# Merge products of two decoder layers taken as three products of split parts instead of one fp32 product

## What is computed

```python
yA = silu(layernorm(conv(...))) @ w_conv_out          # (264 x 512) @ (512 x 1024)
yB = (rmsnorm(o) * silu(z)) @ w_delta_out             # (264 x 512) @ (512 x 1024)
merged = sigmoid(p_gateA) * yA + sigmoid(p_gateB) * yB
x = x + merged @ w_o                                  # (264 x 1024) @ (1024 x 1024)
x = x + FFN(rmsnorm(x))                               # dense in layer 0, top-2-of-8 experts in layer 1
```

## Time and profile before

| | us |
|---|---|
| median of three runs | 1575.98 |
| the profiled execution | 1574.31 |
| its span in the profile | 1572.5 |
| merge stage, layer 0 (first merge product to first output product) | 224.29 to 263.22 |
| merge stage, layer 1 | 697.01 to 735.95 |

### The profile page before, as it was taken

How to read it: one execution, slowest core, us unless ns; L and a number is a source line. 1 busy time by engine, 2 the same in 40 slices (tenths; PEclk the granted TensorE clock), 3 DMA queues, 4 the chain that set the end, 5 groups by cost and what they waited for, 6 DMA issues and landing times.

```text
span 1572.5 us, 31141 instructions
## 1 busy us (share of the span) xinstructions
PE 1539.2 (98%) x11103; PEld 1398.9 (89%) x11103; DVE 1259.7 (80%) x1813; ACT 964.8 (61%) x1340; POOL 46.0 (3%) x52
## 2 busy tenths in 40 slices
PE   7999899999999999999999999999999999999997
PEld 6989887999998989987898997989979899898995
DVE  5878965655545878965598999989899998998987
ACT  5643442544435643442477777777778777787775
POOL 0000000000000000000060000000000000000000
PEclk9999899999999999899999999999999999999999
DMA  7642224687555642234599999999999999999993
GB/s 278 192 102 68 68 86 162 223 272 245 177 168 173 198 102 68 56 91 169 201 354 390 379 358 373 351 360 359 364 371 350 364 358 365 357 349 375 356 366 114
DMA packets 109040, 397.54 MB, mean 253 GB/s; under 512 B 13617, under 2 KB 13664, under 8 KB 108448
## 3 DMA queue, kind: packets, MB, share of 16 engines
q1 hardware_dynamic: 104608, 376.23, 68.1%
q0 software_dynamic: 4352, 20.20, 4.0%
HBM read 380.94 MB, written 16.43 MB: 253 GB/s over the span
## 4 chain that ended last, share of the span: by engine, by line
PE 90%; DVE 8%; ACT 1%; issue 1%; DMA 0%; SPq 0%; DVEq 0%; ACTq 0%
PE psum L1443 74%; DVE c L1011 3%; PE psum L1665 2%; PE psum L1667 2%; PE psum L1558 1%; PE psum L1566 1%; PE psum L1456 1%; PE psum L1674 1%; PE psum L1835 1%; PE psum L1570 1%; DVE w_lo L894 1%; PE psum L1524 1%; PE psum L1788 1%; PE psum L1464 1%; PE psum L1789 0%
## 5 line engine op out<-in xcount | busy, mean ns | idle before, releaser
L1443 PE MATMUL psum<-w_hi,h_hi 128*96 128x256 f32 x1408 | 399.9, 284 | 0.9 <-DVE w_lo L1381 0.9
L1443 PE MATMUL psum<-w_hi,h_lo 128*96 128x256 f32 x1408 | 394.5, 280 | 0.0
L1443 PE MATMUL psum<-w_lo,h_hi 128*96 128x256 f32 x1408 | 393.7, 280 | 0.0
L1381 DVE TENSOR_TENSOR w_lo<-ring,w_hi 128x1024 fp32r<-128x1024 f32 x288 | 346.7, 1221 | 37.2 <-ACT w_hi L847 35.1
L847 ACT ACTIVATE w_hi<-ring 128x1024 fp32r<-128x1024 f32 x288 | 303.6, 1058 | 42.9 <-PE psum L1443 34.0
L1443 PE MATMUL psum<-hid_hi,w_hi 128*128 128x264 f32 x1072 | 312.6, 292 | 1.0 <-DVE hT L1197 0.8
L1443 PE MATMUL psum<-hid_lo,w_hi 128*128 128x264 f32 x1072 | 306.4, 286 | 0.0
L1443 PE MATMUL psum<-hid_hi,w_lo 128*128 128x264 f32 x1072 | 306.0, 285 | 0.0
L582 ACT ACTIVATE w_hi<-ring 128x1024 fp32r<-128x1024 f32 x156 | 164.2, 1056 | 162.8 <-PE psum L1443 123.3
L894 DVE TENSOR_TENSOR w_lo<-ring,w_hi 128x1024 fp32r<-128x1024 f32 x156 | 189.3, 1218 | 92.5 <-ACT w_hi L582 92.3
L1381 DVE TENSOR_TENSOR w_lo<-early,w_hi 128x1024 fp32r<-128x1024 f32 x192 | 231.3, 1221 | 17.9 <-ACT w_hi L847 17.8
(11 more groups left out here) (335 smaller groups left out, 1958.1 us busy)
## 6 DMA issues: line engine op xcount, KB each, us to landing
ring<-in_w_exp SPq DMA_DIRECT2D x288, 512.0 KB, 5.5
early<-in_w_exp SPq DMA_DIRECT2D x192, 512.0 KB, 5.4
ring<-in_w_mixer SPq DMA_DIRECT2D x112, 512.0 KB, 3.6
ring<-in_w_ffn SPq DMA_DIRECT2D x66, 512.0 KB, 4.5
qkv<-in_w_exp SPq DMA_DIRECT2D x48, 512.0 KB, 5.6
h_rows<-work POOLq DMA_DIRECT2D x12, 480.0 KB, 5.1
early<-in_s POOLq DMA_DIRECT2D x2, 2048.0 KB, 8.3
out_ss<-early POOLq DMA_DIRECT2D x2, 2048.0 KB, 9.4
```

Source lines behind the costliest of these rows:

```text
L1381: V.tensor_tensor(w_lo[:, buffer_x(u), :], slot_x(u % RING_X), w_hi[:, buffer_x(u), :], ALU.subtract).then_inc(lo_done, 1)
L1443: last = M(out, lhs[x], rhs[w], start=(start and n == 0), stop=(stop and n == 2))
```

## The change

The eight merge tiles of each layer join the split tiles. ACT makes high parts of `c` (a second silu with a reduced output, ahead of the one in place) and of `o` (four copies), DVE makes their low parts, in work space that is free by then. High and low parts of tiles 40 to 47 are made as of any other tile, three ahead, so that in every turn of the merge loop ACT now makes the high part of tile 43 + t and DVE its low part at the end of the turn. PE takes 24 split products a tile in place of 16 full ones, and waits at its first two merge tiles only for the gates whose banks they overwrite (37 for the first, 39 for the second), and at each tile of `c` and `o` for its low part.

```diff
--- before.py
+++ after.py
@@ -172,6 +172,19 @@
 
         def glu_gate(j):
             return work[:, 8, (j % 2) * T:(j % 2 + 1) * T]
+
+        mix_a = work_r[:, 5:8, :].rearrange("p a b -> p (a b)")
+        mix_b = work_r[:, 0:2, :].rearrange("p a b -> p (a b)")
+
+        def o_part(lo, h):
+
+            return mix_a[:, (4 * lo + h) * T:(4 * lo + h + 1) * T]
+
+        def c_part(lo, j):
+
+            if lo and j == 3:
+                return mix_a[:, 8 * T:9 * T]
+            return mix_b[:, (4 * lo + j) * T:(4 * lo + j + 1) * T]
 
         vmask = units(4)
         sq_o = work[:, 0:2, :].rearrange("p a b -> p (a b)")[:, 0:H * T].rearrange("p (h t) -> p h t", t=T)
@@ -317,6 +330,9 @@
         ln_var = sem("ln_var")
         ln_norm = sem("ln_norm")
         c_done = sem("c_done")
+        o_hi_done = sem("o_hi_done")
+        c_lo_done = sem("c_lo_done")
+        o_lo_done = sem("o_lo_done")
         merged_done = sem("merged_done")
         x_done = sem("x_done")
         silu_done = sem("silu_done")
@@ -382,9 +398,9 @@
 
 
         split_ord = {}
-        for section, tiles in (("mix0", [i for i in range(N_PROJ) if i not in PLAIN]), ("mix0", range(N_PROJ + N_MIX, N_LAYER)),
+        for section, tiles in (("mix0", [i for i in range(N_PROJ) if i not in PLAIN]), ("mix0", range(N_PROJ, N_LAYER)),
                                ("ffn", range(2, N_FFN)),
-                               ("mix1", [i for i in range(N_PROJ) if i not in PLAIN]), ("mix1", range(N_PROJ + N_MIX, N_LAYER))):
+                               ("mix1", [i for i in range(N_PROJ) if i not in PLAIN]), ("mix1", range(N_PROJ, N_LAYER))):
             for i in tiles:
                 split_ord[first_position(section) + i] = len(split_ord)
         split_at = {v: k for k, v in split_ord.items()}
@@ -717,8 +733,7 @@
                             act.wait_ge(qconv_done, 6 * (l + 1))
                             act.wait_ge(qk_state_out, 16 * 2 * (l + 1))
                         A(gs[:, t, :], psum[:, (GATE_AT + t) % 4, 0:T], ACT.Sigmoid).then_inc(act_evac, 1)
-                        if GATE_AT + t + LEAD < N_PROJ:
-                            high_part(section, GATE_AT + t + LEAD)
+                        high_part(section, GATE_AT + t + LEAD)
 
                 z_silu(0)
                 silu_qkv(4, 8)
@@ -764,14 +779,17 @@
                 warm(ACT.Silu)
                 for j in range(CT):
                     act.wait_ge(ln_norm, CT * l + j + 1)
+                    A(c_part(0, j), c[:, j, :], ACT.Silu, scale=par("ln_g", l * CT + j), bias=par("ln_b", l * CT + j))
                     A(c[:, j, :], c[:, j, :], ACT.Silu, scale=par("ln_g", l * CT + j), bias=par("ln_b", l * CT + j)).then_inc(c_done, 1)
+                act.wait_ge(o_done, l + 1)
+                for h in range(H):
+                    A(o_part(0, h), qkv[:, 8 + h, :], ACT.Copy).then_inc(o_hi_done, 1)
                 gates(14, 16)
 
                 for k in range(KD):
                     act.wait_ge(merged_done, KD * l + k + 1)
                     A(x_hi[:, k, :], hT[:, k, :], ACT.Copy).then_inc(x_hi_done, 1)
-                    if k < LEAD:
-                        high_part(f"mix{l}", N_PROJ + N_MIX + k)
+                    high_part(section, N_PROJ + LEAD + k)
                 for t in range(LEAD, N_WO):
                     high_part(f"mix{l}", N_PROJ + N_MIX + t)
                 if l:
@@ -1188,6 +1206,15 @@
                 o_all = qkv[:, 2 * H:3 * H, :]
                 settle(V.scalar_tensor_tensor(o_all, o_all, par("o_g", l), psum[:, 4:8, 0:T], ALU.mult, ALU.mult))
                 V.tensor_tensor(o_all, o_all, zs[:, :, :], ALU.mult).then_inc(o_done, 1)
+                low_part(section, N_PROJ)
+                for j in range(CT):
+                    dve.wait_ge(c_done, CT * l + j + 1)
+                    V.tensor_tensor(c_part(1, j), c[:, j, :], c_part(0, j), ALU.subtract).then_inc(c_lo_done, 1)
+                for h in range(H):
+                    dve.wait_ge(o_hi_done, H * l + h + 1)
+                    V.tensor_tensor(o_part(1, h), qkv[:, 8 + h, :], o_part(0, h), ALU.subtract).then_inc(o_lo_done, 1)
+                for t in range(1, LEAD):
+                    low_part(section, N_PROJ + t)
                 dve.wait_ge(s0_scaled, l + 1)
 
                 for t in range(KD):
@@ -1200,8 +1227,7 @@
                     dve.wait_ge(outer_mm, 8 * l + t + 1)
                     blk = s0[:, 4 * t:4 * t + 4, :].rearrange("p u d -> p (u d)")
                     V.tensor_tensor(blk, blk, psum[:, 6 + t % 2, :], ALU.add).then_inc(outer_taken, 1)
-                    if t >= KD - LEAD:
-                        low_part(f"mix{l}", N_PROJ + N_MIX + t - KD + LEAD)
+                    low_part(section, N_PROJ + LEAD + t)
                 x_low(3 * l + 1, KD - 1)
                 for t in range(KD):
                     dve.wait_ge(units_used, base_ord[f"mix{l}"] + N_PROJ + N_MIX + t + 1)
@@ -1653,18 +1679,18 @@
                 spread(o_rstd, H, 0)
                 project(38)
                 project(39)
-                pe.wait_ge(act_evac, 32 * (l + 1))
-
-                pe.wait_ge(o_done, l + 1)
-                pe.wait_ge(c_done, CT * (l + 1))
                 for t in range(KD):
-                    w = arrived(section, N_PROJ + t)
-                    if t >= 2:
+                    w = parts(section, N_PROJ + t)
+                    if t < 2:
+                        pe.wait_ge(*freed(l, N_PROJ - 3 + 2 * t))
+                    else:
                         pe.wait_ge(merged_done, KD * l + t - 1)
                     for j in range(CT):
-                        M(psum[:, 2 * (t % 2), 0:T], w[:, j, :], c[:, j, :], start=(j == 0), stop=(j == CT - 1))
+                        pe.wait_ge(c_lo_done, CT * l + j + 1)
+                        split_products(psum[:, 2 * (t % 2), 0:T], [x[:, j, :] for x in w], [c_part(0, j), c_part(1, j)], j == 0, j == CT - 1)
                     for h in range(H):
-                        last = M(psum[:, 2 * (t % 2) + 1, 0:T], w[:, CT + h, :], qkv[:, 8 + h, :], start=(h == 0), stop=(h == H - 1))
+                        pe.wait_ge(o_lo_done, H * l + h + 1)
+                        last = split_products(psum[:, 2 * (t % 2) + 1, 0:T], [x[:, CT + h, :] for x in w], [o_part(0, h), o_part(1, h)], h == 0, h == H - 1)
                     last.then_inc(units_used, 1)
                     if t == 0:
                         pe.wait_ge(samp_vm, l + 1)
```

## The result

The changed kernel takes 1565.67 us as the median of eight runs (1561.6 to 1569.62), the kernel before 1576.12 (eight runs, 1573.58 to 1580.13): a ratio of 0.9926 (95% interval 0.9912 to 0.9939), or 9.6 to 13.9 us less. On another occasion, on one chip with three further kernels, it was 1566.16 against 1577.56 us, 0.9932 (0.9913 to 0.9952). The forecast was 1566.8 us, 9.2 less. The profiled span fell from 1572.5 to 1563.2 us.

What follows compares the result with a forecast made beforehand. PE was taken to bound the merge stages, with the DVE-ACT loop narrowly setting their end after the change. 2 x 4.6 = 9.2 us off the profiled 1574.31 gives 1565.1; the median's 1.67 more makes 1566.8 us, range 1563.5 to 1571.5.

Steps and rivals of the forecast that it cites:

- PE's part: Merge tile on PE: 2.90 us split products, 0.20 switching, 1.05 outer product, 4.15 us in all instead of 4.80.
- The bound of 4.46: Upper bound for PE's merge tile, with both the 0.20 us and the 0.31 us switching costs counted.
- The start: First merge tiles: the 0.48 us wait for the last gate goes; the second tile begins 0.5 us late, at 228.2.
- rival (c): Late start: ACT's table switch behind the copies takes twice 1.28 us, everything behind comes 1.3 us later; 1569.4 us, chance 0.02.
- The loop: Merge turns: DVE's merge, ACT's `x_hi` and high part, DVE's low part make a 3.93 us round that sets the end.
- rival (e): Slower: DVE's 0.94 us falls behind ACT's high part, round 4.87; stage loses from 4.6 on; 1580.0 us, chance 0.06.
- Narrowly: End of merge: the DVE-ACT round, done at 258.2 us, sets the end rather than PE, which would allow 257.5.
- The first output tile: Behind the merge: starts at 258.2 us, 5.0 earlier, but waits 0.4 us for the last `x_lo`.
- The sum: Both merge stages: 4.6 us a layer, 9.2 us in all, giving 1566.8 us.
- Rival (a): PE's products alone decide: 0.85 us comes back in each of 16 merge tiles, 13.6 us, 1562.4 us; chance 0.08.
- Rival (d): Given back: something behind the merge, a load or the norm, keeps its own time; 1576 us, chance 0.06.

Runs made afterwards that it cites:

- split outer: Changed kernel with high part ahead of the merge, second tile's high part and last `x_lo` earlier, outer product as three split products; 1566.08 us, 0.9923 to the kernel before.
- the copies inside: Changed kernel plus two 256-column ACT copies in every merge turn, between `x_hi` and the high part; 1577.6 us, 0.9999 to the kernel before.
- the short outer product: Changed kernel with the outer product cut to 128 of 512 columns, rest of the state update left out; 1568.8 us, 0.995 to the kernel before.
- the shorter wait alone: Kernel before with only the shorter wait for gates at the first two merge tiles, products left whole; 1578.98 us, 1.0002 to the kernel before.

## Why the prediction was right

**PE's part.** 4.15 us a tile was taken, with 0.20 for switching and the outer product's 1.05 as it stood. Where PE sets the pace the runs show 4.14 to 4.18. The 0.20 was right as a price, but not as one of switching between full and split products, as split outer shows. The bound of 4.46 rests on a miscount: a merge tile held eight full products and not 16, since each shows as two records, so that one takes 3.75/8 = 0.47 us (and three of split parts, 0.36, three quarters of that). The full product of the earlier trace rows, with 0.54, is 0.07 over that and not 0.31. The 4.15 does not use this term.

**The start.** No wait at the first tile, 0.5 us at the second, DVE's first merge 1.1 us later than before: the runs show none, 0.39 us of idle time, and the first merge 13.47 us behind the spread where it was 12.46, 1.0 later. PE's timeline of the changed kernel, layer 1:

```profile
693.09 1.12 PE L1700 MATMUL psum<-work,rows 32*128 32x512 f32 x2
694.60 0.52 PE L1469 MATMUL psum<-work_r,w_hi 128*128 128x264 f32 x2 [0.39 <-DVE w_lo L912]
```

The silus were 0.5 us each, and the table load took 1.28, so that rival (c) had no place. The Trainium skill (ScalarE: Activation LUTs, What ACT_TABLE_LOAD costs) puts a drain of 1.38 us beside each load. The trace shows none here either: in layer 0 the copies of `o` end at 223.31, the load runs from 223.33 for 1.28 us, and the gate starts at 224.63. ACT's waits on landing, 18.0 us in the earlier trace rows, are gone from both merge stages, as forecast.

**The loop.** 3.93 us a round was the sum, 3.93 to 3.94 is measured. DVE's timeline, layer 1, one turn, beside the earlier trace rows:

```profile
711.42 0.42 DVE L1222 TENSOR_TENSOR gs<-gs,psum 128x264 f32<-128x264 f32 x1
...
714.22 1.23 DVE L912 TENSOR_TENSOR w_lo<-ring,w_hi 128x1024 fp32r<-128x1024 f32 x1 [0.50 <-ACT w_hi L598]
715.36 0.42 DVE L1222 TENSOR_TENSOR gs<-gs,psum 128x264 f32<-128x264 f32 x1
```

The 0.50 us ahead of the low part were said to be 0.57, so `x_lo` and the addition do lie beside ACT's high part: rival (e) is out, and the copies inside the round show that its price was real. At a round of 4.55 the whole gain was gone; the point named was 4.6, though part of that loss was the lower clock behind PE's wait, which (e) did not have. "Narrowly" was right too: the loop ends the stage with a whole clock, PE with a stretch at the lower one.

**The first output tile.** It starts 42.4 us behind the spread with a whole clock, where it was 47.46: 5.0 earlier, as forecast. It waits for the last `x_lo` as forecast too. PE's timeline of the changed kernel, second profile, layer 0, at the start of that tile and at its last products:

```profile
258.71 0.39 PE L1469 MATMUL psum<-hid_hi,w_hi 128*128 128x264 f32 x1 [0.90 <-DVE hT L1224]
...
261.22 0.28 PE L1469 MATMUL psum<-hid_hi,w_lo 128*128 128x264 f32 x1
261.72 0.39 PE L1469 MATMUL psum<-hid_hi,w_hi 128*128 128x264 f32 x1 [0.21 <-DVE hid_lo L918]
```

The idle time is 0.21 us, but the two starts are 0.50 apart instead of 0.12, and from its first product to the addition on DVE the tile takes 3.67 us where it took 3.21 (263.22 to 266.43): the wait costs 0.46, where 0.4 was forecast.

**The sum.** 4.6 us a layer against 4.55 to 4.58 with a whole clock. Rival (a), 13.6 us, is refuted by the copies inside and the short outer product. Rival (d) as well: 24.4, 201.5 and 35.5 us behind the stages didn't move. Each of the two profiled executions has only one such stage, and the two stages together give 8.5 us. That the profiled spans differ by 9.3, so near to 9.2, is luck: 0.8 comes from pieces that the change doesn't touch. There stretches of half clock come and go, and the same piece differs by some 1.5 us from one execution of the changed kernel to the other. The prediction had no term for them; it took the full clock of the earlier trace rows as given, and after the change it is 0.96 in one of the two stages. The measured 10.4 us between the medians is 1.2 more than the sum, and the first interval begins at 9.6, just past it; the second (0.9913 to 0.9952) holds it. That these stretches make up the 1.2 us is likely and not shown.

## What to carry to other kernels

Where work moves from the bounding engine to two others, write out the loop that it closes between them: who hands what to whom in one turn. Its length, and not the engines' busy shares, says whether the cover holds; here a round of 3.93 us decided at an ACT that was idle for 2.56 of them. And write down when that loop starts: this one is shorter than PE's tile and still ended the stage, because its first turn came late. When the stage has come down to where the two are level, taking more off one alone gains little or loses, as here a wait of PE of over 4 us was followed by a lower clock (the short outer product alone); taking it off both went on gaining (stages of 41.88 us). And the whole time then has to be read by pieces, since a gain of a few us in one of them can be lost to the clock in another.

## What was not expected of the hardware

A stretch at the lower level (0.50, 1.2 GHz; 218.3 to 221.7 us in the first profile) came up in the middle of gapless split products, behind the spread of o's norm, in some executions and layers and not in others, and also at the same place in a kernel whose merge products are whole (a mean of 0.97 in stage 0 of the kernel with the shorter wait alone). In the first profile PE had no idle time ahead of it: it was busy for 13.30 of 13.30 us from 205.0 to 218.3. Such a stretch costs a stage 0.6 us where the round of DVE and ACT sets the pace and hides the rest (46.7 against 46.1), and 1.5 where PE does (46.23 against 44.69). And less work for PE made a stage longer: 48.08 and 47.16 us with the short outer product, against 46.1 to 46.8.
